# First modulation groups: half of the blocks as TensorE weights, bias rows for two heads at once, x loaded first

## The chip, the cores and the metric

One of the eight cores of a Trainium2 chip runs the whole kernel; the others are idle. The time is the device time of one launch in microseconds (us). Three runs of the kernel before stand here, and one more execution was taken with a profile.

## What is computed

A transformer block followed by a second block, batch 1, 512 tokens, width 1024, all in float32. What touches the change is the start of the first block and one table of the second:

```
mods = split(silu(c) @ w_ada + b_ada, 9)      # c: [1, 1024], w_ada: [1024, 9216]
sh1, sc1, gt1, sh2, sc2, gt2, sh3, sc3, gt3 = mods
h = rms_norm(x, g_ffn1) * (1 + sc1) + sh1     # x: [512, 1024]
x = x + 0.5 * gt1 * swiglu(h, w1_gu, w1_down) # then mixer, second FFN, ...
# second block: a bias per head and distance
head_bias = rel_bias[:, rel_bucket(dist)]     # rel_bias: [8 heads, 32 buckets]
```

## The kernel before

**Layout.** Activations are kept feature-major: x is 8 tiles of 128 features by 512 tokens. Weights come in blocks of 1 MiB (128 x 2048 floats). Each block is split by ScalarE into a high part w_hi (fp32r, the reduced form of float32) and by VectorE into the rest w_lo; activations are split the same way, and TensorE multiplies hi x hi, hi x lo and lo x hi (`block_fm`, three multiplications of 512 columns for each of 16 weight tiles of a block). Each engine runs its own hand-written list in order, with semaphores between them; SyncE (SP) issues the large loads, ScalarE's queue the small ones.

**Modulation.** w_ada is 36 blocks of 1 MiB, four for each of the nine groups of mods; a block holds two of the eight row tiles t of a group, each 128 x 1024. VectorE (`ada_block`, L1592) does, for each row tile, `ada_acc += block[:, u, :] * c_act[:, t]` over 128 x 1024 numbers. When a group's eight steps are done, TensorE adds up the 128 rows (`ada_columns`): for each of 8 columns j of mods it takes a 128 x 128 piece of ada_acc as weights and a single column of ones as the moving operand, which gives 128 sums in one column of PSUM bank 7. The first two groups (sh1 and sc1, blocks 0 to 7) are needed before the first FFN can begin; their eight blocks go to places of their own (`ada_slots`, over memory that other tensors use later: slots 0 to 3 lie under the split activations act_hi and act_lo, 4 and 5 under w_lo, 6 and 7 are ada_raw). The other seven groups are taken inside the first FFN's loops.

**The start, engine by engine.** SP waits for the two small bias loads, then issues blocks 0 to 3, x (2 MiB), blocks 4 to 7, the first two weight blocks, the constants, and ada block 8 once VectorE has let go of ada_raw (`next_ada`, L440 waits on ada_step). ScalarE computes c_act, copies the bias rows out of PSUM (below), squares the 8 tiles of x, takes the root, makes w_hi of the first block, issues eight DMAs that write the bias rows to DRAM, and then prenorm. VectorE adds squares (`add_squares`), does the 16 modulation steps, inverts the root, makes w_lo of the first block, then `modulation` (adds b_ada), gains and `prenorm`. TensorE makes the bias rows, the statistics, the two `ada_columns`, and then waits for the first tile of prenorm to start the FFN.

**Statistics** (`stats`). The sums of squares over 1024 features: 12 multiplications with a 128 x 128 piece of squares as weights and one column of ones, then the root (ScalarE) and its reciprocal (VectorE), four multiplications of 128 columns that spread the result over the partitions, and three more of 128 columns on ones and zeros (`keep_warm`).

**Bias rows.** For each of 8 heads TensorE multiplies relb (33 x 128: the head's 32 bucket values and a one, the same in all columns) by selector (33 x 640), in two pieces of 512 and 128 columns, float32, into two PSUM banks; two heads' banks are in use by turns. ScalarE copies each to a biasrow tile.

Nearly every matmul of the kernel is issued by the helper at L494, so a row is told by its tiles. A float32 multiplication (both operands float32) shows as two LDWEIGHTS and two MATMUL records, so 8 of them are x16.

Of the kernel before, what the change touches and what calls it, by code (L numbers as in the profile page):

```python
# [23 lines left out]
P = 128  # L24
S = 512
# [88 lines left out]
def build(nc, ten):  # L114
    ctx = ExitStack()
    with ctx:
        def sem(name):
            return ctx.enter_context(nc.semaphore(name))

        def alloc(stack, name, shape, dt=F32):  # L120
            return stack.enter_context(nc.sbuf_tensor(name, shape, dt))
# [52 lines left out]
        with ExitStack() as s:  # L174
            selector = alloc(s, "selector", [33, NDIST])
            rel = alloc(s, "rel", [33, 8])
            relb = alloc(s, "relb", [33, 8, P])
            biasrow = [alloc(s, f"biasrow{h}", [P, NDIST]) for h in range(8)]
# [85 lines left out]
        def col(name, i=0, n=1):  # L264
            return cols[:, CAT[name] + i:CAT[name] + i + n]
# [18 lines left out]
        ada_zero = sem("ada_zero")  # L284
# [142 lines left out]
        def _(sp):  # L427
# [15 lines left out]
            def next_ada(b, k):  # L443
                sp.wait_ge(ada_step, 2 * b - 2)
                load_ada(b, k)
# [7 lines left out]
            sp.wait_ge(rel_in, 16)  # L453
            sp.wait_ge(sel_in, 16)
            for b in range(4):
                load_first(b)
            sp.dma_start(x[:], ten["x"]).then_inc(x_in, 16)
            for b in range(4, ADA_FIRST):
                load_first(b)
            load(0, 0)  # L460
            load(0, 1)
            sp.dma_start(consts[:, P:], ten["consts"][:, P:]).then_inc(consts_in, 16)
            next_ada(ADA_FIRST, 0)
# [26 lines left out]
        def _(pe):  # L490
# [302 lines left out]
            pe.wait_ge(sel_in, 16)  # L793
            pe.wait_ge(relb_ready, 1)
            for h in range(8):
                if h >= 2:
                    pe.wait_ge(brow_copied, h - 1)
                k = 2 * (h % 2)
                mm(ps[:, k, :], relb[:, h, :], selector[:, 0:S])
                mm(ps[:, k + 1, 0:NDIST - S], relb[:, h, :],  # L800
                   selector[:, S:NDIST]).then_inc(brow_sum, 1)
            pe.wait_ge(ident_in, 16)
            stats()
            for g in range(2):
                ada_columns(g)
# [238 lines left out]
        def _(act):  # L1044
# [147 lines left out]
            act.dma_start(selector[:], ten["selector"]).then_inc(sel_in, 16)  # L1192
            act.dma_start(rel[0:32, :], ten["rel"]).then_inc(rel_in, 16)
            act.dma_start(cols[:], ten["cols"]).then_inc(cols_in, 16)
# [5 lines left out]
            for h in range(8):  # L1200
                act.wait_ge(brow_sum, h + 1)
                k = 2 * (h % 2)
                fn(biasrow[h][:], ps[:, k:k + 2, :].rearrange("p a n -> p (a n)")[:, 0:NDIST]) \
                    .then_inc(brow_copied, 1)
# [6 lines left out]
            act.wait_ge(brow_copied, 8)  # L1211
            for h in range(8):
                act.dma_start(scratch[h], biasrow[h][:]).then_inc(brow_out, 16)
# [237 lines left out]
        def _(dve):  # L1451
# [135 lines left out]
            def ada_start(g):  # L1587
                if g >= 2:
                    dve.wait_ge(ada_sum, g - 1)
                v.memset(ada_acc[g % 2][:], 0.0).then_inc(ada_zero, 1)  # L1590
                dve.wait_ge(ada_zero, g + 1)

            def ada_block(g, i, k):

                slot = ada_raw[k]
                if g < 2:
                    b = 4 * g + 2 * i + k
                    dve.wait_ge(ada_first_in[b], 16)
                    slot = ada_slots[b]
                else:  # L1600
                    dve.wait_ge(ada_in[k], 16 * (2 * g + i - 3))
                for u in range(2):
                    t = 4 * i + 2 * k + u
                    at = slice(t, t + 1) if isinstance(t, int) else bass.ds(t, 1)
                    dve.wait_ge(ada_step, DT * g + t)
                    v.scalar_tensor_tensor(out=ada_acc[g % 2][:], in0=slot[:, u, :],  # L1606
                                           scalar=c_act[:, at], in1=ada_acc[g % 2][:],
                                           op0=ALU.mult, op1=ALU.add).then_inc(ada_step, 1)

# [162 lines left out]
            dve.wait_ge(rel_in, 16)  # L1772
            link(v.memset(rel[32:33, :], 1.0))
            for h in range(8):
                last = v.tensor_scalar(relb[:, h, :], ones[0:33, :], rel[:, h:h + 1], None, ALU.mult)
# [6 lines left out]
            for g in range(2):  # L1782
                ada_start(g)
                for i in range(2):
                    for k in range(2):
                        ada_block(g, i, k)
                    if g == 1 and i == 0:
                        invert()
                if g == 0:
                    for t in range(DT):  # L1790
                        add_squares(t)
            lo(0, 0)
            modulation(0, 2)
            v.tensor_scalar(negsink[:], col("sinks", 0, 16), -1.0, None, ALU.mult)
            gain(0, 1, "g_ffn1").then_inc(mods_ready, 1)
            dve.wait_ge(mods_ready, 1)
            prenorm(gains[:, 0], mods[:, 0:8])
# [604 lines left out]
```

## Time and profile before

| | |
|---|---|
| runs | 2290.36, 2295.14 (median), 2296.44 us |
| profiled execution | 2295.65 us, its span 2293.9 us |
| TensorE matmuls busy | 2204.2 us, 96% of the span |
| VectorE busy | 1157.0 us, 50% |
| ScalarE busy | 737.8 us, 32% |
| mean granted TensorE clock | 0.971 |

The profiled execution is one run of its own; 1.75 us of it lie outside the span. Times in the rows below are counted from the span's start. PE is TensorE, PEld its weight loads (beside its matmuls), DVE is VectorE, ACT is ScalarE, SP is SyncE; a q behind an engine is its sequencer or DMA queue. PEclk is the granted TensorE clock as a share of 2.4 GHz.

### The profile page before, as it was taken

What the parts mean: (1) busy time and instruction counts of PE and PEld (TensorE: products, weight loads), DVE (VectorE), ACT (ScalarE), POOL (GpSimd) and SP (SyncE); (2) the same over time, 40 slices, a digit from 0 to 9 for tenths busy, and PEclk for the clock granted to TensorE, in tenths of its full rate; (3) what the DMA queues carried; (4) which work ended last, traced back from release to release, by engine and by line L of the source; (5) the groups of instructions that cost most, each with busy time, mean ns of one, the idle gap of its engine ahead of it and who ended that gap; (6) DMA issues with size and microseconds to landing.
All of it is one profiled execution on the core that took longest, in us unless ns stands there. A gap on an engine that the chain in (4) does not pass through costs nothing.

```text
span 2293.9 us, 27734 instructions
## 1 busy us (share of the span) xinstructions
PE 2204.2 (96%) x10894; PEld 1790.9 (78%) x10894; DVE 1157.0 (50%) x1863; ACT 737.8 (32%) x1085; POOL 0.2 (0%) x4
## 2 busy tenths in 40 slices
PE   7999999999999999999999999998999899999997
PEld 5888888788887668788888787676688878888886
DVE  7655654645235764533333566655565545333334
ACT  3321212322323652431212344554433424312122
POOL 0000000000000000000000000000000000000000
PEclk9999999999999999999999999998999998999998
DMA  8554443222222112232222224010123121222221
GB/s 347 198 190 181 182 180 114 92 91 92 95 89 74 38 56 92 74 110 92 91 93 101 100 92 166 20 38 19 60 106 111 37 74 57 108 92 91 92 96 70
DMA packets 35314, 234.99 MB, mean 102 GB/s; under 512 B 4347, under 2 KB 4603, under 8 KB 7708
## 3 DMA queue, kind: packets, MB, share of 16 engines
q1 hardware_dynamic: 31968, 227.62, 27.5%
q10 hardware_dynamic: 3260, 6.19, 0.8%
q8 instruction: 58, 0.95, 0.2%
q14 instruction: 28, 0.23, 0.0%
HBM read 229.07 MB, written 4.72 MB: 102 GB/s over the span
## 4 chain that ended last, share of the span: by engine, by line
PE 91%; DVE 6%; ACT 2%; issue 1%; DMA 0%; ACTq 0%; DVEq 0%
PE ps L494 89%; PE ps L729 2%; DVE w_lo L1468 1%; ACT w_hi L1049 1%; ACT pt L1049 1%; DVE act_lo L1510 1%; DVE x L1528 0%; DVE normed L1526 0%; DVE act L1519 0%; DVE ada_acc L1606 0%; DVE normed L1519 0%; DVE act_lo L1508 0%; ACT square L1049 0%; ACT act_hi L1049 0%; ACT L1049 0%
## 5 line engine op out<-in xcount | busy, mean ns | idle before, releaser
L494 PE MATMUL ps<-act_hi,w_hi 128*128 128x512 f32 x1824 | 724.7, 397 | 14.6 <-DVE act_lo L1510 5.6
L494 PE MATMUL ps<-act_lo,w_hi 128*128 128x512 f32 x1824 | 715.0, 392 | 0.0
L494 PE MATMUL ps<-act_hi,w_lo 128*128 128x512 f32 x1824 | 714.6, 392 | 0.0
L1049 ACT ACTIVATE w_hi<-raw 128x2048 fp32r<-128x2048 f32 (+1 forms) x200 | 340.7, 1704 | 319.4 <-PE ps L494 315.4
L1468 DVE TENSOR_TENSOR w_lo<-raw,w_hi 128x2048 fp32r<-128x2048 f32 x168 | 384.6, 2289 | 94.7 <-ACT w_hi L1049 89.5
L494 PEld LDWEIGHTS ps<-act_hi,w_hi 128*128 128x128 f32 x1824 | 345.4, 189 | 96.4 <-issue 15.7
L494 PEld LDWEIGHTS ps<-act_hi,w_lo 128*128 128x128 f32 x1824 | 345.2, 189 | 73.2
L494 PEld LDWEIGHTS ps<-act_lo,w_hi 128*128 128x128 f32 x1824 | 345.7, 190 | 70.7 <-issue 1.0
L494 PE MATMUL ps<-hid_hi,w_hi 128*128 128x512 f32 x656 | 261.3, 398 | 1.7 <-DVE hid_lo L1727 1.7
L494 PE MATMUL ps<-hid_lo,w_hi 128*128 128x512 f32 x656 | 260.3, 397 | 0.0
L494 PE MATMUL ps<-hid_hi,w_lo 128*128 128x512 f32 x656 | 260.2, 397 | 0.0
L1640 DVE TENSOR_TENSOR prod<-silu,ps 128x512 f32<-128x512 f32 x66 | 45.4, 687 | 362.2 <-ACT silu L1049 362.1
L1049 ACT ACTIVATE silu<-ps 128x512 f32<-128x512 f32 x66 | 39.5, 598 | 524.0 <-PE ps L494 524.0
L494 PEld LDWEIGHTS ps<-hid_hi,w_hi 128*128 128x128 f32 x656 | 123.9, 189 | 31.6 <-issue 1.9
L494 PEld LDWEIGHTS ps<-hid_hi,w_lo 128*128 128x128 f32 x656 | 123.9, 189 | 30.2
L494 PEld LDWEIGHTS ps<-hid_lo,w_hi 128*128 128x128 f32 x656 | 123.9, 189 | 29.4
L1049 ACT ACTIVATE pt<-ps 128x512 f32<-128x512 f32 (+5 forms) x84 | 48.2, 574 | 121.0 <-PE ps L729 121.0
L1567 DVE SCALAR_TENSOR_TENSOR x<-ps,gains,x 128x512 f32 (+1 forms) x44 | 31.0, 746 | 105.1 <-PE ps L494 105.1
L1606 DVE SCALAR_TENSOR_TENSOR ada_acc<-ada_raw,c_act,ada_acc 128x1024 f32<-128x1024 f32 x60 | 76.9, 1282 | 6.6 <-DVE ada_acc L1606 2.8
L1049 ACT ACT_TABLE_LOAD x51 | 65.4, 1283 | 4.8 <-issue 3.9
L1649 DVE TENSOR_TENSOR hid_lo<-prod,hid_hi 128x512 f32 (+1 forms) x66 | 45.7, 693 | 7.9
L1049 ACT ACTIVATE square<-x 128x512 f32<-128x512 f32 x42 | 25.7, 624 | 61.5 <-DVE x L1567 35.3
(307 smaller groups left out, 2069.0 us busy)
## 6 DMA issues: line engine op xcount, KB each, us to landing
raw<-in_weights SPq DMA_DIRECT2D x176, 1024.0 KB, 4.9
ada_raw<-in_ada SPq DMA_DIRECT2D x30, 1024.0 KB, 4.9
ada_slot<-in_ada SPq DMA_DIRECT2D x6, 1024.0 KB, 10.7
bias_rows<-biasrow ACTq DMA_DIRECT2D x8, 320.0 KB, 6.9
x<-in_x SPq DMA_DIRECT2D x1, 2048.0 KB, 15.9
table<-bias_rows ACTq DMA_DIRECT2D x1, 2048.0 KB, 8.1
result<-x SPq DMA_DIRECT2D x8, 256.0 KB, 2.0
consts<-in_consts SPq DMA_DIRECT2D x1, 1088.5 KB, 29.2
```

The lines of the kernel that those rows point to most:

```text
L494: return nc.tensor.matmul(out, lhsT, rhs, start=start, stop=stop)
L729: last = nc.tensor.transpose(turned_to(g, w, k + P)[:, a, k:], sc(g)[:, a, k:k + w], ident)
L1049: return nc.scalar.activation(out, in_, func, **kw)
L1468: v.tensor_tensor(w_lo[k][:], raw[k][:], w_hi[k][:].bitcast(F32), ALU.subtract).then_inc(split_lo, 1)
L1510: ins = v.scalar_tensor_tensor(out=act_lo[:, t, :], in0=gained[t % 4], scalar=shift[:, t:t + 1], in1=high, op0=ALU.add, op1=ALU.subtract)
L1567: last = v.scalar_tensor_tensor(out=tile, in0=ps[:, 2 * k + u, :], scalar=gate[:, at], in1=tile, op0=ALU.mult, op1=ALU.add)
L1606: v.scalar_tensor_tensor(out=ada_acc[g % 2][:], in0=slot[:, u, :], scalar=c_act[:, at], in1=ada_acc[g % 2][:], op0=ALU.mult, op1=ALU.add). ...
L1640: v.tensor_tensor(prod[k][:], silu[k][:], ps[:, 2 * k + 1, :], ALU.mult).then_inc(block_used, 1)
L1649: v.tensor_tensor(lo_tile, prod[k][:], hi_tile.bitcast(F32), ALU.subtract).then_inc(hid_ready, 1)
```

## The change

- relb, rel and selector get a second copy in partitions 64 to 96. Even heads use partitions 0 to 32, odd heads 64 to 96. TensorE issues the four pieces of two heads alternately, into four banks; two pairs' banks are in use by turns. ScalarE still copies head by head.
- The second copies are loaded by SP, which waits for both copies of both. x is loaded first, then blocks 0 to 6, the first weight block, block 7, the second weight block. The eight bias-row stores move from ScalarE's queue to SP's; ada block 8 goes ahead of the constants, behind them.
- Of the eight first modulation blocks VectorE takes 1, 3, 5 and 6; a group's first step is a plain product in place of a memset and a multiply-add. TensorE takes 0, 2, 4 and 7 (`ada_direct_block`): the 128 x 128 pieces of the block as they came from DRAM are the weights, the column of c_act is the moving operand, 16 multiplications for a block, all added up in bank 7. What VectorE has summed is added to the same columns as before (`ada_sums`).
- TensorE's order becomes: bias rows; wait for all eight copies; blocks 0 and 2; statistics; block 4; ada_sums of both groups; block 7; FFN.
- VectorE's order becomes: block 1; squares; block 3; reciprocal; blocks 5 and 6; wait for TensorE's third block; w_lo; wait for the fourth; modulation, gains, prenorm. negsink moves behind the gains.

```diff
-            selector = alloc(s, "selector", [33, NDIST])
-            rel = alloc(s, "rel", [33, 8])
-            relb = alloc(s, "relb", [33, 8, P])
+            selector = alloc(s, "selector", [97, NDIST])
+            rel = alloc(s, "rel", [97, 8])
+            relb = alloc(s, "relb", [97, 8, P])
...
-        ada_zero = sem("ada_zero")
+        ada_zero, ada_direct = sem("ada_zero"), sem("ada_direct")
...
                     .then_inc(ada_first_in[b], 16)
-            sp.wait_ge(rel_in, 16)
-            sp.wait_ge(sel_in, 16)
-            for b in range(4):
-                load_first(b)
+            sp.dma_start(rel[64:96, :], ten["rel"]).then_inc(rel_in, 16)
+            sp.dma_start(selector[64:97, :], ten["selector"]).then_inc(sel_in, 16)
+            sp.wait_ge(rel_in, 32)
+            sp.wait_ge(sel_in, 32)
             sp.dma_start(x[:], ten["x"]).then_inc(x_in, 16)
-            for b in range(4, ADA_FIRST):
+            for b in range(ADA_FIRST - 1):
                 load_first(b)
             load(0, 0)
+            load_first(ADA_FIRST - 1)
             load(0, 1)
+            sp.wait_ge(brow_copied, 8)
+            for h in range(8):
+                sp.dma_start(scratch[h], biasrow[h][:]).then_inc(brow_out, 16)
+            next_ada(ADA_FIRST, 0)
             sp.dma_start(consts[:, P:], ten["consts"][:, P:]).then_inc(consts_in, 16)
-            next_ada(ADA_FIRST, 0)
             late = (ADA_BLOCKS - ADA_FIRST) // 2
             with sp.Fori(1, late) as p:
...
                 pe.wait_ge(filled, 1)
                 mm(ps[:, 6, k:k + 1], ones[:], ones[:, 0:1]).then_inc(block_done, 1)
-            pe.wait_ge(sel_in, 16)
+            pe.wait_ge(sel_in, 32)
             pe.wait_ge(relb_ready, 1)
-            for h in range(8):
-                if h >= 2:
-                    pe.wait_ge(brow_copied, h - 1)
-                k = 2 * (h % 2)
-                mm(ps[:, k, :], relb[:, h, :], selector[:, 0:S])
-                mm(ps[:, k + 1, 0:NDIST - S], relb[:, h, :],
-                   selector[:, S:NDIST]).then_inc(brow_sum, 1)
+            for pair in range(4):
+                if pair >= 2:
+                    pe.wait_ge(brow_copied, 2 * pair - 2)
+                k = 4 * (pair % 2)
+                for first, end in ((0, S), (S, NDIST)):
+                    for u in range(2):
+                        rows = slice(64 * u, 64 * u + 33)
+                        last = mm(ps[:, k + 2 * u + first // S, 0:end - first],
+                                  relb[rows, 2 * pair + u, :], selector[rows, first:end])
+                last.then_inc(brow_sum, 1)
+
+            def ada_sums(g):
+
+                pe.wait_ge(ada_step, 4 * (g + 1))
+                for j in range(DT):
+                    last = mm(ps[:, 7, g * DT + j:g * DT + j + 1], ada_acc[g][:, j * P:j * P + P],
+                              ones[:, 0:1], False, False)
+                return last
+
+            def ada_direct_block(b):
+
+                pe.wait_ge(ada_first_in[b], 16)
+                for u in range(2):
+                    t = 2 * (b % 4) + u
+                    for j in range(DT):
+                        at = DT * (b // 4) + j
+                        last = mm(ps[:, 7, at:at + 1], ada_slots[b][:, u, j * P:j * P + P],
+                                  c_act[:, t:t + 1], False,
+                                  b == ADA_FIRST - 1 and u == 1 and j == DT - 1)
+                last.then_inc(ada_direct, 1)
+
+            pe.wait_ge(brow_copied, 8)
+            pe.wait_ge(c_ready, 1)
+            mm(ps[:, 7, 0:2 * DT], zeros[:, 0:P], ones[:, 0:2 * DT], True, False)
+            ada_direct_block(0)
+            ada_direct_block(2)
             pe.wait_ge(ident_in, 16)
             stats()
-            for g in range(2):
-                ada_columns(g)
+            ada_direct_block(4)
+            ada_sums(0).then_inc(ada_sum, 1)
+            ada_sums(1).then_inc(ada_sum, 1)
+            ada_direct_block(7)
             ffn(0, AT["ffn1"], 0)
...
                 outs(g1 - 1)
-            act.dma_start(selector[:], ten["selector"]).then_inc(sel_in, 16)
             act.dma_start(rel[0:32, :], ten["rel"]).then_inc(rel_in, 16)
+            act.dma_start(selector[0:33, :], ten["selector"]).then_inc(sel_in, 16)
             act.dma_start(cols[:], ten["cols"]).then_inc(cols_in, 16)
             act.dma_start(ident, ten["consts"][:, 0:P]).then_inc(ident_in, 16)
             for e, name in enumerate(("w2k", "w2v")):
...
             act.wait_ge(cols_in, 16)
             fn(c_act[:], col("c", 0, DT), ACT.Silu).then_inc(c_ready, 1)
             for h in range(8):
-                act.wait_ge(brow_sum, h + 1)
-                k = 2 * (h % 2)
+                act.wait_ge(brow_sum, h // 2 + 1)
+                k = 2 * (h % 4)
                 fn(biasrow[h][:], ps[:, k:k + 2, :].rearrange("p a n -> p (a n)")[:, 0:NDIST]) \
                     .then_inc(brow_copied, 1)
             act.wait_ge(x_in, 16)
...
                 squares(t, x[:, t, :])
             take_root()
             hi(0, 0)
-            act.wait_ge(brow_copied, 8)
-            for h in range(8):
-                act.dma_start(scratch[h], biasrow[h][:]).then_inc(brow_out, 16)
             act.wait_ge(mods_ready, 1)
             prenorm(mods[:, 0:8])
             ffn(AT["ffn1"], x)
...
                 if g >= 2:
                     dve.wait_ge(ada_sum, g - 1)
                 v.memset(ada_acc[g % 2][:], 0.0).then_inc(ada_zero, 1)
-                dve.wait_ge(ada_zero, g + 1)
+                dve.wait_ge(ada_zero, g - 1)
             def ada_block(g, i, k):
                 slot = ada_raw[k]
-                if g < 2:
-                    b = 4 * g + 2 * i + k
-                    dve.wait_ge(ada_first_in[b], 16)
-                    slot = ada_slots[b]
-                else:
-                    dve.wait_ge(ada_in[k], 16 * (2 * g + i - 3))
+                dve.wait_ge(ada_in[k], 16 * (2 * g + i - 3))
                 for u in range(2):
                     t = 4 * i + 2 * k + u
                     at = slice(t, t + 1) if isinstance(t, int) else bass.ds(t, 1)
...
                     v.scalar_tensor_tensor(out=ada_acc[g % 2][:], in0=slot[:, u, :],
                                            scalar=c_act[:, at], in1=ada_acc[g % 2][:],
                                            op0=ALU.mult, op1=ALU.add).then_inc(ada_step, 1)
+
+            def ada_first_block(b, steps):
+
+                dve.wait_ge(ada_first_in[b], 16)
+                acc = ada_acc[b // 4]
+                for u in range(2):
+                    t = 2 * (b % 4) + u
+                    if steps % 4 == 0 and u == 0:
+                        ins = v.tensor_scalar(acc[:], ada_slots[b][:, u, :], c_act[:, t:t + 1], None,
+                                              ALU.mult)
+                    else:
+                        dve.wait_ge(ada_step, steps + u)
+                        ins = v.scalar_tensor_tensor(out=acc[:], in0=ada_slots[b][:, u, :],
+                                                     scalar=c_act[:, t:t + 1], in1=acc[:],
+                                                     op0=ALU.mult, op1=ALU.add)
+                    ins.then_inc(ada_step, 1)
             def modulation(first, end):
...
             v.memset(zeros[:], 0.0)
             v.memset(eps[:], EPS).then_inc(filled, 1)
             dve.wait_ge(filled, 1)
-            dve.wait_ge(rel_in, 16)
-            link(v.memset(rel[32:33, :], 1.0))
+            dve.wait_ge(rel_in, 32)
+            v.memset(rel[32:33, :], 1.0)
+            link(v.memset(rel[96:97, :], 1.0))
             for h in range(8):
-                last = v.tensor_scalar(relb[:, h, :], ones[0:33, :], rel[:, h:h + 1], None, ALU.mult)
+                rows = slice(64 * (h % 2), 64 * (h % 2) + 33)
+                last = v.tensor_scalar(relb[rows, h, :], ones[rows, :], rel[rows, h:h + 1], None,
+                                       ALU.mult)
             last.then_inc(relb_ready, 1)
             for k in range(START):
                 v.memset(nmx[k][:], 0.0).then_inc(block_used, 1)
             dve.wait_ge(c_ready, 1)
-            for g in range(2):
-                ada_start(g)
-                for i in range(2):
-                    for k in range(2):
-                        ada_block(g, i, k)
-                    if g == 1 and i == 0:
-                        invert()
-                if g == 0:
-                    for t in range(DT):
-                        add_squares(t)
+            ada_first_block(1, 0)
+            for t in range(DT):
+                add_squares(t)
+            ada_first_block(3, 2)
+            norms[0] += 1
+            dve.wait_ge(root_ready, norms[0])
+            v.reciprocal(rinv[:, 0:NT], root[:, 0:NT]).then_inc(rinv_ready, 1)
+            ada_first_block(5, 4)
+            ada_first_block(6, 6)
+            dve.wait_ge(ada_direct, 3)
             lo(0, 0)
+            dve.wait_ge(ada_direct, 4)
             modulation(0, 2)
-            v.tensor_scalar(negsink[:], col("sinks", 0, 16), -1.0, None, ALU.mult)
             gain(0, 1, "g_ffn1").then_inc(mods_ready, 1)
+            v.tensor_scalar(negsink[:], col("sinks", 0, 16), -1.0, None, ALU.mult).then_inc(ada_step, 8)
             dve.wait_ge(mods_ready, 1)
+            dve.wait_ge(rstd_ready, norms[0])
             prenorm(gains[:, 0], mods[:, 0:8])
             dve.wait_ge(brow_out, 16 * 8)
             ffn(AT["ffn1"], gains[:, 3], ada=True)
```

## Rows read from the trace of the kernel before

**Rows 1.** The page: span; busy time of each engine; shares of the chain that ended last.
```profile
span 2293.9 us, 27734 instructions
PE 2204.2 (96%) x10894; PEld 1790.9 (78%) x10894; DVE 1157.0 (50%) x1863; ACT 737.8 (32%) x1085; POOL 0.2 (0%) x4
PE 91%; DVE 6%; ACT 2%; issue 1%; DMA 0%; ACTq 0%; DVEq 0%
```
**Rows 2.** The chain of waits, 0 to 120 us: start, us, what.
```profile
4.95 17.42 PE ps L494 x32
...
40.75 1.30 DVE ada_acc L1606
...
42.09 3.59 PE ps L494 x16
...
45.91 0.17 DVE negsink L1794
...
46.19 0.76 DVE normed L1519
...
62.17 57.91 PE ps L494 x254
```
**Rows 3.** Timeline of PE, 28 to 49 us: start, us, instruction, count.
```profile
28.09 1.87 PE L494 MATMUL ps<-ones,sumsq 128*128 128x1 f32 x8 [5.22 <-DVE sumsq L1485]
29.82 3.55 PE L494 MATMUL ps<-ones,square 128*128 128x1 f32 x16
34.60 2.08 PE L494 MATMUL ps<-consts,rinv 128*128 128x128 f32 x8 [1.23 <-DVE rinv L1499]
...
37.75 2.27 PE L494 MATMUL ps<-ones,ada_acc 128*128 128x1 f32 x16
...
48.69 0.77 PE L494 MATMUL ps<-act_hi,w_hi 128*128 128x512 f32 x1 [3.02 <-DVE act_lo L1510]
```
**Rows 4.** Busy time by stretch: us, PE, PEld, DVE, ACT, POOL, PEclk, DMA share, GB/s.
```profile
5.00:22.00 17.00, 17.00 (x32) 8.68 (x32) 11.19 (x9) 5.13 (x8) 0.00 (x0) 1.00 1.01 421
28.40:31.80 3.40, 3.40 (x18) 3.40 (x17) 3.28 (x3) 1.25 (x4) 0.00 (x0) 1.00 1.01 422
...
38.60:42.00 3.40, 1.43 (x13) 1.34 (x12) 3.26 (x4) 0.00 (x0) 0.00 (x0) 1.00 1.04 408
42.00:45.40 3.40, 3.31 (x16) 3.31 (x16) 2.24 (x2) 0.00 (x0) 0.00 (x0) 0.51 1.04 420
...
48.80:52.30 3.50, 3.50 (x9) 2.73 (x10) 3.50 (x6) 1.87 (x3) 0.00 (x0) 0.50 0.76 318
```
**Rows 5.** The same view, 1888 to 1899 us, where TensorE only adds up squares.
```profile
1888.60:1892.00 3.40, 1.63 (x15) 1.46 (x14) 3.30 (x6) 1.26 (x2) 0.00 (x0) 1.00 0.02 5
...
1895.40:1898.80 3.40, 3.40 (x18) 3.40 (x17) 3.30 (x6) 1.63 (x4) 0.00 (x0) 0.50 0.01 2
```
**Rows 6.** Timeline of PE at 754 us, partitions 0-63 and 64-127: two score multiplications.
```profile
754.15 0.39 PE L494 MATMUL ps<-k_hi,hid_hi 64*128 64x256 f32 x2
```
**Rows 7.** The tile k_hi: nanoseconds of one, min/median/max, of all 64 such.
```profile
L494 PE MATMUL ps<-k_hi,hid_hi x64: 323/383/579, 737.2 to 831.0; 64*128 64x256 f32 x48, 64*128 64x128 f32 x16
```
**Rows 8.** Timeline of ACT, 7 to 23 us: the last copy of a bias row.
```profile
22.39 0.70 ACT L1049 ACTIVATE biasrow<-ps 128x640 f32<-128x640 f32 x1 [1.43 <-PE ps L494]
```
**Rows 9.** Timeline of SP, 0 to 12 us: the issues of two loads.
```profile
5.05 0.44 SPq L457 DMA_DIRECT2D x<-in_x  x1
...
9.67 2.12 SPq L462 DMA_DIRECT2D consts<-in_consts  x1
```
**Rows 10.** The page's DMA issues; the last number is us from issue to landing.
```profile
x<-in_x SPq DMA_DIRECT2D x1, 2048.0 KB, 15.9
...
consts<-in_consts SPq DMA_DIRECT2D x1, 1088.5 KB, 29.2
```
**Rows 11.** Timeline of DVE, 56 to 63 us: low part of the second weight block.
```profile
59.82 2.29 DVE L1468 TENSOR_TENSOR w_lo<-raw,w_hi 128x2048 fp32r<-128x2048 f32 x1 [1.40 <-ACT w_hi L1049]
```

## Prediction

> **What bounds the kernel now.** I read the page first: of a span of 2293.9 us TensorE's matmuls are busy for 2204.2, and the chain that ended last lies on TensorE for 91% [rows 1]. Once the first FFN has begun, TensorE hardly stops, and nothing of the change touches what it does there. So the change is worth the shift of one moment: the first FFN matmul, at 48.69 us [rows 3]. What comes after should follow that moment us for us.
>
> Then the chain of waits over the first 120 us [rows 2]. It starts with TensorE's bias rows, 17.42 us without a gap, goes through the squares and VectorE's modulation steps, the last of which begins at 40.75 and takes 1.30, then TensorE's 3.59 us of column sums for the second group, the small VectorE work, and prenorm from 46.19 on. The reader is to see that two engines take turns, and that VectorE holds the chain from about 28 to 42 us. The change takes work from VectorE and gives it to TensorE.
>
> Last, the timeline of TensorE and its busy time by stretch, for the price of that work. A multiplication with a 128x128 float32 weight tile and a single moving column shows as two records. From 28.09 to 29.82 us there are 8 records [rows 3], four multiplications in 1.73 us, 0.43 us each. From 42.09 on, 16 records take 3.57 us, again 0.43 to 0.45 us each. [rows 4] give the clock of that stretch as 0.51 of full speed, the 1.2 GHz level. From 38.6 to 42.0 it is at 1.00, the 2.4 GHz level, and the 16 records that begin at 37.75 take only 2.27 us in all. Up to 38.6 us the clock column reads 1.00 as well, but the same operation has the slow spacing there, so I read the start of the kernel as the 1.2 GHz level that was not written down.
>
> **The change part by part.**
>
> *Bias rows for two heads at once.* At 754 us two multiplications of 256 columns on partitions 0-63 and 64-127 take 0.39 us together [rows 6], where one alone has a median of 0.383 [rows 7]. So they run side by side, and I take half of 17.42 us: 8.7 saved on TensorE. Bounds: 0 if float32 pieces on 33 rows don't overlap; about 11.5 if the clock rises on the way, since then ScalarE's copies, 8 x 0.70 us [rows 8], become the limit. The second copies of rel and selector ride in a second queue. I put 0.3 us on the start for them (an estimate; between 0 and 1 us). TensorE starts at 5.25, ends the rows at 13.95, and waits for the last two copies, 1.4 us: 15.35.
>
> *TensorE's blocks.* Four blocks of 16 multiplications are new: 64 x 0.432 = 27.6 us. The 16 multiplications of the two column sums stay, 6.9 us, and both now stand in one row with the rest. Bounds for one multiplication: 0.43 at the low clock, 0.22 (half) at the high. I take the low one because of [rows 5]: from 1895.4 to 1898.8 TensorE does nothing but such multiplications, its matmuls and its weight loads are each busy for 3.40 of 3.40 us, and the clock is 0.50; in the stretch from 1888.6, with 15 such records, it still reads 1.00, and it has fallen by the next one. The stretch from 28.4 to 31.8, just as full, doesn't raise it either [rows 3, 4]. So this kind of work neither raises the clock nor keeps it.
>
> The Trainium skill ("TensorE: Matmul & The Clock Gate", the section "Why this matters for your kernels") advises keeping TensorE continuously busy to have and hold the full clock. By that rule the new order, almost without idle time, would run at 2.4 GHz, and the result would be the first rival below; here [rows 5] disagree, 3.40 us busy of 3.40 at 0.50. The skill's "TensorEngine Tiling (Array Packing)", under "Instruction Overhead", puts a matmul with one moving column at about 60 cycles. That would be an estimate of 4.0 us for all 80 at 1.2 GHz, and again the first rival's time. The rows show 0.43 us for each, as the weight load has to be paid, so the measured value stands.
>
> *Statistics.* They lie between blocks 2 and 4: 13 multiplications of the same kind, 5.6 us; root and reciprocal 0.6 (1.23 in [rows 3], where VectorE was first busy with a modulation step, which it isn't now); spreading and keep_warm, 34.60 to 37.75, 3.15 us. Sum 9.35.
>
> *VectorE's part.* Eight steps instead of 16, less two memsets. Blocks 1 and 3 and the squares are over long before TensorE has done block 2; blocks 5 and 6 need 4 x 1.30 = 5.2 us after the reciprocal and are ready before TensorE reaches the column sums. All of it is hidden beside TensorE. Without that cover (first rival) they would still end before block 7 is in. w_lo of the first block (about 2.3 us, as in [rows 11]) waits for TensorE's third block and lies beside the column sums. negsink leaves the chain, 0.17 us and its hand-over [rows 2]: 0.2.
>
> *Loads.* x lands at 5.05 + 15.9 = 20.95 us as the last of 6 MiB, the constants at 9.67 + 29.2 = 38.9 as the last of 13.06 [rows 9, 10]: 2.54 us per MiB. Now x is in after 2 MiB and block 7 is the eleventh: 20.95 + 5 x 2.54 + 0.3 to 0.7 = 34 us or a little later. Blocks 0 and 2 land (3rd and 5th MiB) at about 14 and 19, before TensorE wants them. What SP issues later is moved too: eight bias-row stores, then ada block 8, which now waits until negsink, then the constants, and behind them the weight block for the third FFN block. From that wait these are 3.1 MiB, about 10 us with latency, and the third block's w_hi is wanted only when the first FFN block has been multiplied, some 13 us after prenorm begins. Ada block 8 is first read at about the same time. I cost this at nothing; if the margin of about 4 us were gone, it would be paid once. The stores leave ScalarE's queue while ScalarE waits anyway: nothing.
>
> *The sum.* 15.35 + 0.43 (the zero that opens the bank) + 13.8 (blocks 0, 2) + 9.35 + 6.9 (block 4) + 6.9 (column sums) + 6.9 (block 7) = 59.6, +0.15 for the end of the last one; before, it was 3.0 us from the end of the column sums (42.09 + 3.59) to the first FFN matmul, now 2.8. The FFN starts at 62.6 instead of 48.7: 13.9 us later with a low clock throughout.
>
> Against this stands one stretch at the high clock. Spreading and keep_warm raised it at 38.6 us before, for 3.4 us [rows 4]; the same work is now followed at once by block 4, which would do 6.8 us of slow work in those 3.4. I take this once: 10.5 us late. It need not come (high end 13.9), and the paired bias rows might raise the clock as well, which one head at a time did not in 17 us [rows 4]; that would give back up to 1.5 in the rows (their last 3 us at half the time) and 3.4 behind them (low end 5.6). A lower clock at the FFN's start was there before, with 0.50 to 52.3 [rows 4], and its second block waited for w_lo until 62.11 [rows 11], so about 0.6 us of a worse start is free.
>
> Own execution before 2295.65 us (span and 1.75 around it) + 10.5 = 2306. It stands 0.5 us above the median of the runs, 2295.14.
>
> **The rivals.**
>
> 1. *Faster: TensorE runs the blocks at the high clock, and the loads bound the start.* With the sum's terms at half, 15.35 + 0.2 + 6.9 + 5.0 + 3.5 + 3.5, all before block 7 is done by about 34; block 7 lands there, 16 x 0.216 = 3.5, + 2.8: FFN at 40.6, 8.1 us earlier, 2287.6. It decides where 13.9 of the 17.3 us between the two prices of 80 multiplications are saved, at 0.26 us for one. For it: less idle time on TensorE, and VectorE's steps from 28 to 42 us are gone. Against it: [rows 5]. 0.08.
>
> 2. *No difference: two or three stretches at the high clock,* in the bias rows' end, block 0, and after the statistics. 13.9 less 7 to 11: 2298.5 to 2302.5. For it: twice as many rows of the array at work in the paired stretch. Against it: [rows 4, 5]. 0.22.
>
> 3. *The pairs do not run side by side.* 8.7 us more: 2314.9. Against it [rows 6, 7]; for it only that those are fp32r. 0.03.
>
> **How the numbers follow.** The forecast (2302.5 to 2310.5) gets 0.67. A difference of 0.3%, 6.9 us, is about what a measurement of this kernel tells from none: faster is below 2288.3, slower above 2302.0. Faster 0.08 (rival 1), same 0.23 (rival 2 and the edge of the forecast), slower 0.69. The range reaches into rival 2, and up to the sum with no high clock plus the runs' spread: 2297 to 2311.
>
> **What would show it.** Right: first FFN matmul at 57 to 63 us; bias rows over by 14; an unbroken row of one-column multiplications with a clock of 0.50 but for one stretch; VectorE waiting for TensorE before w_lo. Wrong: block 7's multiplications beginning when its load lands; PEclk 1.00 in the blocks; bias rows lasting 17 us; a gap in TensorE between the first and third FFN block, from the late loads.

## The result

Slower, by 0.66%. Four runs of the changed kernel have a median of 2309.98 us (2306.36 to 2311.79), four of the kernel before 2295.43 (2290.36 to 2296.44); the ratio is 1.0066, 95% interval 1.0045 to 1.0086. The profiled execution took 2308.24 us, its span is 2306.0. The median lies inside the range (2297 to 2311) and 4 us above the forecast of 2306, where the sum of the prediction comes out without a stretch at the high clock (2295.65 + 13.9 = 2309.5).

The page of the changed kernel: TensorE has 17 us more of busy time in a span that is 12 us longer, and x now lands 8.0 us after its issue instead of 15.9 [rows 1, 10].

```profile
span 2306.0 us, 27986 instructions
PE 2221.6 (96%) x11024; PEld 1813.7 (79%) x11024; DVE 1144.7 (50%) x1854; ACT 737.7 (32%) x1085; POOL 0.2 (0%) x4
...
x<-in_x SPq DMA_DIRECT2D x1, 2048.0 KB, 8.0
```

Its chain of waits over the first 120 us (start, us, what), to be held against [rows 2]. VectorE's modulation steps are gone from it. From 15.61 us on it is TensorE alone, but for the root and its reciprocal: 92 and 110 records without a gap.

```profile
5.32 8.92 PE ps L498 x32
...
15.61 19.80 PE ps L498 x92
...
35.97 23.64 PE ps L498 x110
...
62.54 57.53 PE ps L498 x241
```

The timeline of TensorE (start, us, instruction, count, and in brackets idle time before it), the answer to [rows 3]. The reader is to see that each block (32 records) costs 6.83 to 6.97 us, two of them 13.79, and that the first FFN matmul is at 62.54 instead of 48.69.

```profile
16.06 13.79 PE L498 MATMUL ps<-c_act,ada_slot 128*128 128x1 f32 x64
...
30.14 1.85 PE L498 MATMUL ps<-ones,sumsq 128*128 128x1 f32 x8
31.85 3.55 PE L498 MATMUL ps<-ones,square 128*128 128x1 f32 x16
35.97 2.08 PE L498 MATMUL ps<-consts,rinv 128*128 128x128 f32 x8 [0.56 <-DVE rinv L1834]
...
39.12 6.83 PE L498 MATMUL ps<-c_act,ada_slot 128*128 128x1 f32 x32
45.80 6.97 PE L498 MATMUL ps<-ones,ada_acc 128*128 128x1 f32 x32
52.63 6.96 PE L498 MATMUL ps<-c_act,ada_raw 128*128 128x1 f32 x32
62.54 0.77 PE L498 MATMUL ps<-act_hi,w_hi 128*128 128x512 f32 x1 [2.94 <-DVE act_lo L1542]
```

The clock column does not show which level this was: it reads 1.00 over all of it, as it did in the kernel before up to 38.6 us. The spacing does. 65 records in 13.79 us and 98 in 20.30 are 0.21 us each, as in the 16 records of [rows 4] whose clock is given as 0.51, where the high level of [rows 5] has 15 records in 1.63 us. Busy time by stretch of the changed kernel (us, PE, PEld, DVE, ACT, POOL, PEclk, DMA share, GB/s):

```profile
15.60:29.40 13.80, 13.79 (x65) 13.79 (x65) 7.89 (x9) 5.93 (x10) 0.00 (x0) 1.00 1.01 421
39.10:59.40 20.30, 20.30 (x98) 20.30 (x96) 3.74 (x3) 0.00 (x0) 0.00 (x0) 1.00 0.16 65
```

The timeline of VectorE, which held the chain before, now shows two long waits for TensorE:

```profile
45.98 2.29 DVE L1500 TENSOR_TENSOR w_lo<-raw,w_hi 128x2048 fp32r<-128x2048 f32 x1 [5.40 <-PE ps L498]
59.63 0.17 DVE L1657 TENSOR_TENSOR mods<-ps,cols 128x16 f32<-128x16 f32 x1 [11.36 <-PE ps L498]
```

The start is 13.85 us later and the span 12.1 us longer. The shift stays what it is through the first FFN (ScalarE's thirteenth w_hi begins at 188.05 instead of 174.23 us, its twenty-fifth at 325.53 instead of 311.71, 13.8 both times). Most of the 1.7 us that come back do so between 806 and 926 us, in code that the change does not touch: the kernel before had a low-clock stretch there and this execution had not. The same 342 or 343 TensorE records in the two, busy time by stretch, before and then changed:

```profile
845.00:925.00 80.00, 80.00 (x342) 65.08 (x342) 36.35 (x32) 23.42 (x21) 0.00 (x0) 0.98 0.26 92
```

```profile
858.00:937.00 79.00, 79.00 (x343) 64.35 (x343) 36.59 (x32) 23.53 (x21) 0.00 (x0) 1.00 0.27 93
```

Another execution of the changed kernel (below) ended 15.8 us behind the one of before with the same 13.8 at the start. The other profiles drift more: split and wide is 3.0 us ahead at the first FFN matmul and 11.4 at the end (span 2282.5), one head at a time 21.6 behind and 18.0 at the end (span 2311.9). So the end of one profile carries several us either way that the start did not put there. The experiments are read at the first FFN matmul, which has one profile for each kernel (the changed kernel and x late have two each, and the four lie within 0.02 us), and a median is not explained to better than a few us.

### The profile page after: what moved, and what is told of

It is laid out like the page before. It is cut to its first block, busy times and chain, and to the rows that moved or that the text cites. A ratio compares the mean times of both kernels' runs of the same rounds, so it can differ in the third digit from the quotient of the medians.

```text
span 2306.0 us, 27986 instructions
## 1 busy us (share of the span) xinstructions
PE 2221.6 (96%) x11024; PEld 1813.7 (79%) x11024; DVE 1144.7 (50%) x1854; ACT 737.7 (32%) x1085; POOL 0.2 (0%) x4
## 4 chain that ended last, share of the span: by engine, by line
PE 93%; DVE 4%; ACT 2%; issue 1%; DMA 0%; ACTq 0%; DVEq 0%
PE ps L498 91%; PE ps L733 2%; DVE w_lo L1500 1%; ACT pt L1084 1%; ACT w_hi L1084 1%; DVE x L1560 0%; DVE normed L1558 0%; DVE normed L1551 0%; DVE act_lo L1540 0%; DVE act_lo L1542 0%; ACT act_hi L1084 0%; DVE act L1551 0%; ACT square L1084 0%; DMA raw<-in_weights 0%; ACT L1084 0%
## 5 line engine op out<-in xcount | busy, mean ns | idle before, releaser
L1633 DVE SCALAR_TENSOR_TENSOR ada_acc<-ada_raw,c_act,ada_acc 128x1024 f32<-128x1024 f32 x56 | 71.8, 1282 | 4.7 <-DVE ada_acc L1633 3.3
```

## Experiments

The theory: the first FFN matmul is set by TensorE's chain, above all 80 multiplications with a single moving column, each 0.427 us since the clock is low. Rivals: the new order of the loads costs the time; the pairs of bias rows do; the price of a block is the moving data's and not the weight load's.

The fourth column is the median of the kernel before, timed in the same session as the run.

| kernel | first FFN matmul, us | median, us | before beside it | ratio (95%) |
|---|---|---|---|---|
| before | 48.69 | | | |
| changed | 62.54 | 2309.98 | 2295.43 | 1.0066 (1.0045-1.0086) |
| no blocks on TensorE | 45.76 | 2291.64 | 2292.76 | 0.9990 (0.9980-1.0000) |
| two blocks | 45.84 | 2293.55 | 2292.76 | 0.9998 (0.9984-1.0012) |
| one head at a time | 70.31 | 2314.97 | 2292.76 | 1.0086 (1.0066-1.0106) |
| wide | 45.10 | 2289.61 | 2292.76 | 0.9983 (0.9973-0.9994) |
| split and wide | 45.68 | 2289.31 | 2294.30 | 0.9976 (0.9967-0.9985) |
| x late | 62.52 | 2305.76 | 2294.30 | 1.0045 (1.0030-1.0061) |
| split, one column | 48.93 | 2294.74 | 2294.30 | 0.9997 (0.9986-1.0008) |
| wide statistics | 45.05 | 2287.47 | 2294.85 | 0.9971 (0.9959-0.9983) |
| changed again | 62.52 | 2307.78 | 2294.85 | 1.0055 (1.0040-1.0071) |
| x late again | 62.52 | 2307.89 | 2294.85 | 1.0055 (1.0040-1.0071) |
| clock held | 43.52 | 2284.33 | 2292.94 | 0.9962 (0.9946-0.9979) |

**No blocks on TensorE.** Everything else as changed; VectorE takes all eight blocks.

```diff
-            ada_direct_block(0)
-            ada_direct_block(2)
             stats()
-            ada_direct_block(4)
             ada_sums(0).then_inc(ada_sum, 1)
             ada_sums(1).then_inc(ada_sum, 1)
-            ada_direct_block(7)
# VectorE: block 0, squares, 1, 2, reciprocal, 3, 4, 5, 6, 7, w_lo
```

> The changed kernel with one part undone: VectorE takes all eight first blocks (16 steps), TensorE none. Paired bias rows, x first and SP's queue stay. Theory (TensorE's chain of slow one-column multiplications sets the start): bias rows over at 14.2 as in the changed kernel, VectorE's steps end at about 39.5 (block 0 in at about 14, 16 steps of 1.29, squares 3.9), column sums of the second group 3.5, 2.8 to the first FFN matmul: 46, against 48.7 before and 62.5 changed. Time some 2.5 us below the kernel before, 16 below the changed one. Rival (the order of the loads or the bias stores in SP's queue costs the time): the first FFN matmul stays at 60 or later, since the queue is unchanged.

Measured: 45.76, where 46 was expected. TensorE's timeline has its old wait for VectorE back:

```profile
29.77 3.41 PE L498 MATMUL ps<-ones,ada_acc 128*128 128x1 f32 x16
39.24 3.57 PE L498 MATMUL ps<-ones,ada_acc 128*128 128x1 f32 x16 [6.06 <-DVE ada_acc L1645]
45.76 0.77 PE L498 MATMUL ps<-act_hi,w_hi 128*128 128x512 f32 x1 [2.94 <-DVE act_lo L1539]
```

The whole loss is the direct blocks; the rest of the change (paired rows, x first, the plain products, the moved stores) starts the FFN 2.9 us sooner together. What each of these is worth was not separated; the median gained only 1.1 us. The rival of the loads is out, since the queue is the changed one.

**Two blocks.**

```diff
             ada_direct_block(0)
             ada_direct_block(2)
             stats()
-            ada_direct_block(4)
             ada_sums(0) ... ada_sums(1)
-            ada_direct_block(7)
# VectorE: block 1, squares, 3, 4, 5, 6, reciprocal, 7, w_lo
```

> The changed kernel, but TensorE multiplies only blocks 0 and 2; VectorE takes 1, 3, 4, 5, 6, 7. Theory: TensorE's chain loses 2 x 6.83 = 13.7 us of multiplications that stood after the statistics, nothing else takes their place (VectorE's last step ends near 38.5, the first group's column sums near 42.6): first FFN matmul at 62.5 - 13.7 = 48.9, time within 2 us of the kernel before. Rival (loads): no change against the changed kernel. A rival that the price comes from only one of the blocks, the last (waiting for its load), gives 55.7.

Measured: 45.84, 3.1 us better than the 48.9 expected, and the timeline says by what: both column sums took 3.72 us where the changed kernel has 6.97. This execution had the high-clock stretch behind the statistics that the forecast had counted on. Up to 39.11 us its TensorE timeline is that of the changed kernel to 0.01 us, and neither of the two profiles of the changed kernel has the stretch. So the order of the work alone does not decide it, and an execution can have it or not. The median over ten runs, 0.8 us above the kernel before, fits 48.9 better than 45.8, but its interval excludes neither.

```profile
39.11 3.72 PE L498 MATMUL ps<-ones,ada_acc 128*128 128x1 f32 x32
45.84 0.77 PE L498 MATMUL ps<-act_hi,w_hi 128*128 128x512 f32 x1 [3.01 <-DVE act_lo L1541]
```

**One head at a time.**

```diff
-                        rows = slice(64 * u, 64 * u + 33)
+                        rows = slice(0, 33)
# and relb computed in partitions 0 to 32 for all heads
```

> The changed kernel with the bias rows one head at a time: all heads use the copies in partitions 0 to 32, the multiplications keep their order and their banks. Theory: the rows take 17.1 us again instead of 8.9, all of it on the chain: first FFN matmul at 70.6, time 8 us above the changed kernel. Rival (the pairs are hidden behind loads or copies): no change.

Measured: 70.31; the rows took 17.41 us instead of 8.90, and all of it reached the FFN, less 0.7 that the rows began earlier.

```profile
4.60 17.41 PE L498 MATMUL ps<-selector,relb 33*128 33x512 f32 x32 [2.25 <-DVE relb L1821]
...
70.31 0.77 PE L498 MATMUL ps<-act_hi,w_hi 128*128 128x512 f32 x1 [2.94 <-DVE act_lo L1543]
```

So the pairs do run side by side, in float32 and on 33 rows too, and save 8.5 us, where the sum had 8.7.

**Wide.** The same multiplications, 128 equal moving columns each.

```diff
-    last = mm(ps[:, 7, at:at + 1], ada_slots[b][:, u, j * P:j * P + P], c_act[:, t:t + 1], ...)
+    last = mm(ps[:, at // 4, (at % 4) * P:(at % 4) * P + P], ada_slots[b][:, u, j * P:j * P + P],
+              c_act[:, t:t + 1].to_broadcast([P, P]), ...)
# the same in ada_sums; mods read ps[:, 0:4, 0:512:128]
```

> The changed kernel with 128 equal moving columns in place of one in every modulation multiplication (blocks 0, 2, 4, 7 and the column sums): each c_act column, and the ones in the column sums, is repeated 128 times; the sums land in PSUM banks 0 to 3, 128 equal columns for each of the 16 results, and VectorE reads every 128th. The number and the weights of the multiplications are the same. Theory (the multiplications are bound by their float32 weight loads at 0.213 us a record at 1.2 GHz, and one moving column keeps the clock low): the same 0.213 at the start, then the clock rises and a record takes 0.107 to 0.112; blocks 0 and 2 over by 24 to 27 instead of 29.7, everything after the statistics in about half of 20.5 us: first FFN matmul between 46 and 53. Rival (moving columns are what costs, so 128 of them cost more): each record above 0.213 and the FFN later than 62.5. Rival (the clock follows only how long TensorE is busy, not what it does): no change, 62.5.

Measured: 45.10, 17.4 us earlier than with one column, by doing 128 times the streaming. Blocks 0 and 2 took 9.00 us instead of 13.79, block 7 3.74 instead of 6.96. The first 13 records, to 18.4 us, still have the slow spacing (the changed kernel has 13 up to there as well); in the next 3.4 us there are 30, then 34. The statistics in between are the old one-column ones, and after them the clock is low again for a while (0.59), then back. TensorE's timeline, and its busy time by stretch:

```profile
15.62 9.00 PE L498 MATMUL ps<-c_act,ada_slot 128*128 128x128 f32 x64 [1.39 <-ACT biasrow L1092]
...
30.03 4.98 PE L498 MATMUL ps<-c_act,ada_slot 128*128 128x128 f32 x32
34.85 3.73 PE L498 MATMUL ps<-ones,ada_acc 128*128 128x128 f32 x32
38.42 3.74 PE L498 MATMUL ps<-c_act,ada_raw 128*128 128x128 f32 x32
45.10 0.48 PE L498 MATMUL ps<-act_hi,w_hi 128*128 128x512 f32 x1 [2.94 <-DVE act_lo L1550]
```

```profile
18.40:21.80 3.40, 3.40 (x30) 3.40 (x30) 3.07 (x5) 2.02 (x4) 0.00 (x0) 1.00 1.02 429
21.80:25.20 3.40, 3.40 (x34) 3.40 (x32) 3.17 (x3) 2.39 (x4) 0.00 (x0) 1.00 1.02 424
...
28.60:32.00 3.40, 3.40 (x21) 3.40 (x21) 3.26 (x3) 0.00 (x0) 0.00 (x0) 0.59 1.01 422
```

It settles two rivals. 128 moving columns cost no more than one: 13 records at the low level either way, and at the high one 32 records in 3.73 us here and in 3.72 with a single column (two blocks). That leaves the weight load as the price. And being busy is not what decides the clock: the one-column blocks kept PE and PEld busy for 20.30 of 20.30 us at the slow spacing. The wide version also writes to banks 0 to 3 instead of bank 7; that was not tested by itself.

The Trainium skill ("TensorE: Matmul & The Clock Gate", "Why this matters for your kernels") advises keeping TensorE continuously busy. The 128-column blocks bear that out, the one-column blocks do not. A stream of columns is not the whole answer either: the kernel before streams its bias rows, 512 and 128 columns on 33 partitions, for 17.42 us without a gap [rows 2], and the two records right behind them take 0.59 us, where the same two take 0.28 behind the wide blocks. Which property of the wide blocks raised the clock stays open. Timeline of PE in the kernel before, then in wide:

```profile
22.28 0.59 PE L494 MATMUL ps<-ones,zeros 128*128 128x4 f32 x2
```

```profile
24.46 0.28 PE L498 MATMUL ps<-ones,zeros 128*128 128x4 f32 x2
```

**Split and wide.** A version meant to be better than both kernels.

```diff
+            ada_direct_block(0), stats(), ada_direct_block(5)
+            ada_sums(0); keep_warm(12); ada_sums(1)
# VectorE: block 1, squares, 2, reciprocal, 3, 4, 6, 7, w_lo; all moving operands 128 wide
```

> Paired rows, x first, 128 equal moving columns as in the wide run, and another split: TensorE multiplies blocks 0 (ahead of the statistics) and 5 (behind them), VectorE blocks 1, 2, 3, 4, 6, 7; twelve idle 128-column multiplications stand between the two groups' column sums, to fill TensorE's wait for VectorE. Theory: VectorE sets the end, with 12 steps, squares and one wait for the root done at 37 to 37.5; the last column sums then take 1.9 at the high clock (3.5 at the low), 2.85 to the first FFN matmul: 41.7 to 43.7, some 5 to 7 us below the kernel before. Rival (TensorE still sets it, the clock having fallen in the statistics): block 5 ends at 36, column sums at the low clock: 45 to 46, no gain over the wide run.

Measured: 45.68; the expectation missed by 2 to 4 us. Its rival gave the number (45 to 46) and was right that TensorE still set the start: in the one-column statistics the clock fell and stayed low until block 5. It was wrong about the sums, which ran at the high level, 1.95 us each. VectorE began w_lo at 38.07, its last step done, but TensorE reached the last sums only at 40.72, behind the twelve idle multiplications, which had become part of the chain.

```profile
38.04 2.84 PE L498 MATMUL ps<-zeros,ones 128*128 128x128 f32 x24
40.72 1.95 PE L498 MATMUL ps<-ones,ada_acc 128*128 128x128 f32 x16
```

```profile
25.20:28.60 3.40, 2.83 (x13) 2.75 (x14) 0.85 (x3) 0.27 (x1) 0.00 (x0) 0.50 1.02 422
28.60:32.00 3.40, 3.40 (x17) 3.40 (x17) 3.33 (x4) 0.00 (x0) 0.00 (x0) 0.50 1.00 414
```

**Split, one column.** The same split without the wide operands and the idle multiplications.

> The split of the run above with a single moving column everywhere and without the idle multiplications. It tells the split from the clock. Theory: block 0 from 15.6 to 29.4 halved to 22.4, statistics to 32, block 5 6.8, two column sums 6.8 at 1.2 GHz: 45.7, less up to 3.4 if a high-clock stretch comes; first FFN matmul between 45 and 48.6. Rival (the split alone does it, the clock is a detail): 42 to 43.

Measured: 48.93, a little over the top of the expected 45 to 48.6, as no high-clock stretch came: block 5 took 6.83 us, the two sums 6.96. The split alone is worth 13.6 us over the changed kernel and nothing over the kernel before.

```profile
32.26 6.83 PE L498 MATMUL ps<-c_act,ada_slot 128*128 128x1 f32 x32
38.95 6.96 PE L498 MATMUL ps<-ones,ada_acc 128*128 128x1 f32 x32
48.93 0.77 PE L498 MATMUL ps<-act_hi,w_hi 128*128 128x512 f32 x1 [3.02 <-DVE act_lo L1541]
```

**x late,** twice, the second time beside the changed kernel on the same chip.

```diff
+            for b in range(4): load_first(b)
             sp.dma_start(x[:], ten["x"]).then_inc(x_in, 16)
-            for b in range(ADA_FIRST - 1): load_first(b)
+            for b in range(4, ADA_FIRST - 1): load_first(b)
```

> The changed kernel with x at its old place in SP's queue, behind blocks 0 to 3; all else as changed. Theory: TensorE is the chain from 15.6 us on and has 14 us of block work before it wants the squares, so x landing at about 22 in place of 11 changes nothing: first FFN matmul at 62.5, time within 2 us of the changed kernel. Rival (loading x first delays the blocks and costs time): several us faster than the changed kernel.

The first FFN matmul is at 62.52, the same. The median, 2305.76, lay 4.2 below the changed kernel's, where I had expected at most 2. The two had been timed in different sessions, so both were run once more side by side:

> The changed kernel itself, to have it on the same chip and beside the same runs as the one below. Its first FFN matmul at 62.5 again, or up to 3.4 earlier if a high-clock stretch comes behind the statistics.

> The changed kernel with x at its old place in SP's queue once more, beside the changed kernel itself. Theory: the same first FFN matmul and the same time within 1.5 us. Rival (x first costs something that the profile of one run does not show): 3 to 4 us faster than the changed kernel.

Measured: 2307.78 and 2307.89, both ratios 1.0055, both first FFN matmuls at 62.52. The first difference did not come back, and medians of four runs each scatter by that much. x first is worth nothing while TensorE is the chain.

**Wide statistics.** Split and wide, with the statistics' twelve sums 128 columns wide too and no idle multiplications.

```diff
-    last = mm(ps[:, 4, i:i + 1], src[:, i * P:i * P + P], ones[:, 0:1], ...)
+    last = mm(ps[:, 4, i * P:i * P + P], src[:, i * P:i * P + P], ones[:, 0:P], ...)
-    keep_warm(WARM)   # behind the statistics, and the twelve before the last sums
```

> The split and the 128 equal moving columns of the split-and-wide run, with the statistics' twelve sums of squares made 128 columns wide too (ScalarE takes the root of every 128th), and without keep_warm behind them and without the idle multiplications. Theory: the clock no longer falls in the statistics; they end at about 25.6 instead of 27.7, VectorE's reciprocal comes 1.7 earlier, its last step ends at about 36.5 and w_lo at 38.8, TensorE is done with the last column sums before that or at most at 40: first FFN matmul between 41.7 and 43, 6 to 7 us below the kernel before. Rival (removing keep_warm lets the clock fall before the column sums): 44 to 45.

Measured: 45.05, 2 to 3 us above the expectation and at the rival's 44 to 45. The sums of squares were over at 26.4, where 25.6 was expected. Two further causes show in the profile, VectorE first, then TensorE by stretch: block 7 was not in when VectorE wanted it (it came at 35.6, not at 34.1), 1.50 us; and while TensorE waited 4.79 us for VectorE the clock fell, so that the last sums took 3.78 us.

```profile
35.60 2.61 DVE L1676 SCALAR_TENSOR_TENSOR ada_acc<-ada_raw,c_act,ada_acc 128x1024 f32<-128x1024 f32 x2 [1.50 <-DMA ada_raw<-in_ada]
```

```profile
35.40:38.80 3.40, 0.54 (x2) 0.54 (x3) 3.16 (x3) 0.00 (x0) 0.00 (x0) 0.63 1.01 399
38.80:42.20 3.40, 3.24 (x16) 2.95 (x14) 1.66 (x2) 0.00 (x0) 0.00 (x0) 0.50 1.02 403
```

**Clock held.** The same with `keep_warm(20)` in that wait.

> The run with wide statistics, and twenty idle 128-column multiplications between the two groups' column sums, where TensorE waited 4.8 us for VectorE and the last sums then ran at the low clock, 3.78 us. Theory (the kind of work in the wait decides the clock): the idle multiplications take 4.3 to 4.6 us and end before VectorE's last step at 38.2, the last sums take 1.95, w_lo (ends at 40.4) now comes last: first FFN matmul at 43.2, 1.9 us earlier than without them. Rival (the clock falls by itself there): sums at 3.7, FFN at 45 or later.

Measured: 43.52, where 43.2 was expected, and 2284.33 us, 0.38% below the kernel before (0.21 to 0.54%). It is the lowest median here, though its interval overlaps those of the other wide versions. The last sums took 2.05 us at PEclk 1.00, and w_lo came last, if only by 0.1 us (38.31 + 2.28 against 38.45 + 2.05). The median lies 8.6 us below the kernel before and the start accounts for 5.2; in wide statistics it is 7.4 and 3.6. The rest was not traced: the profiled execution of clock held, the slowest of its seven runs, ends 5.1 us ahead.

```profile
33.09 4.63 PE L498 MATMUL ps<-zeros,ones 128*128 128x128 f32 x40
38.45 2.05 PE L498 MATMUL ps<-ones,ada_acc 128*128 128x128 f32 x16 [0.74 <-DVE ada_acc L1677]
43.52 0.47 PE L498 MATMUL ps<-act_hi,w_hi 128*128 128x512 f32 x1 [3.01 <-DVE act_lo L1571]
```

```profile
38.31 2.28 DVE L1529 TENSOR_TENSOR w_lo<-raw,w_hi 128x2048 fp32r<-128x2048 f32 x1
```

```profile
38.80:42.20 3.40, 1.70 (x16) 1.51 (x14) 3.35 (x6) 0.34 (x1) 0.00 (x0) 1.00 1.04 406
```

## Why the prediction was right, step by step

- *What is worth what.* The whole change is one shift of the first FFN matmul: 13.85 us at 62.54, and 13.8 us at the two later points of the first FFN that were read. Right for the mechanism; behind the first FFN single executions drift by several us.
- *The 0.3 us at the start* came out (5.32 instead of 4.95), but for another reason than the second queue: rel landed 0.44 us earlier, and VectorE's eight products for relb took 0.71 us longer (last section). Luck.
- *Bias rows:* 5.32 to 14.24 against 5.25 to 13.95. Right, and shown by the run with one head at a time. The clock had not risen behind them (13.79 us for the first two blocks).
- *A block at 6.9 us:* 6.83 to 6.97. Right. The 0.43 us for a multiplication holds for the blocks as they came from DRAM as for ada_acc.
- *Statistics 9.35 us:* 29.71 to 39.12, 9.4. Right. *VectorE and the loads hidden:* VectorE waited 5.40 and 11.36 us for TensorE. Right, though block 7 lands about 1.5 us later (at 35.6 in the run with wide statistics, where VectorE waits for it) than the 34 reckoned. *The late loads behind negsink:* no gap of TensorE between the first and the third FFN block (57.53 us of unbroken chain from 62.54 on). Right.
- *One stretch at the high clock, -3.4 us:* this term was wrong. It came in neither of the two profiles of the changed kernel, nor in the two of x late, nor with one head at a time or in the split with one column; it came in the run with two blocks. Left out, the sum gives 62.6 for the first FFN matmul (62.54) and 2309.5 for the time (2309.98). It is most of the 4 us between forecast and median. That the time agrees to 0.5 us is luck: four more runs of the same kernel had a median of 2307.78, 12.9 us above the kernel before beside them instead of 14.6.
- *The signs.* The prediction asked for a clock of 0.50 in the one-column row and named PEclk 1.00 in the blocks as a sign of being wrong. The column did read 1.00 there. It had been read rightly for the kernel before, where 1.00 stood over the slow spacing up to 38.6 us; the sign should have been the spacing, 0.21 us a record, and that came.
- *The rival of the high clock* named the right condition. Once the clock was made to rise (wide), the four blocks on TensorE cost 3.7 to 5 us each, and the FFN began 3.6 us before that of the kernel before, not 8.1. Most of the difference is slow spacing at two places, in block 0 and again behind the statistics. The rival's own sum was loose: its terms add up to 34.45, and with 3.5 and 2.8 us behind that or behind the load at 34 they give 40.3 to 40.8, where it has 40.6. The prediction's estimate of 4.0 us for all 80 multiplications would not give this time either but one near 38, with 0.8 us for block 7 instead of 3.5.

## What to carry to other kernels

Before moving work to an engine that looks idle, price one instruction of it at the clock the engine has there, and add them up in that engine's order: half of the blocks cost 27 us on TensorE, the same half on VectorE 10 (8 steps of 1.30 us). A float32 multiplication with a single moving column cost what one with 128 columns costs, the weight load. A row of such ones stayed at the low clock here (0.21 us a record for 20.30 busy us), while the same multiplications with 128 equal columns brought the clock up. Let idle multiplications fill only a wait, and count that they end before it does: twelve in the wrong place stood in the chain, twenty in a true wait made the start 1.5 us earlier (one profile each).

## What was not expected of the hardware

VectorE's eight small products for relb (33 partitions x 128) took 1.65 us when all stood in partitions 0 to 32 and 2.36 us when they alternated between 0 and 64, 0.7 us ahead of the first bias row. The cause was not looked for. VectorE's timeline of the changed kernel, then that of the run with one head at a time:

```profile
2.81 2.36 DVE L1820 TENSOR_SCALAR relb<-ones,rel 33x128 f32<-33x128 f32 x8
```

```profile
2.80 1.65 DVE L1821 TENSOR_SCALAR relb<-ones,rel 33x128 f32<-33x128 f32 x8
```
